# A hybrid decoder trunk on one core: the token tiles loaded first and by one queue, further expert rows fetched a chunk ahead, and a token's two expert rows summed on TensorE in the first layer

## The chip, the cores and the metric

The kernel runs on one core of a Trainium2 chip. The metric is the device time of one execution in microseconds (us), median over several executions. TensorE (PE), VectorE (DVE), ScalarE (ACT) and GpSimd (POOL) compute; SyncE (SP) issues most DMAs. "PEld" is the load of a matmul's stationary operand, PEclk the clock granted to TensorE as a share of 2.4 GHz. An fp32 matmul shows in the trace as two records.

## What is computed

One inference step of a two-layer trunk over 544 tokens (512 of a prompt, 32 of eight sample streams) with 1024 channels in fp32, cut to what matters here:

```python
for layer in (0, 1):
    h = rms_norm(x, g_mix[layer])
    x = x + (even_mixer(h) if layer == 0 else odd_mixer(h))  # attention + short conv; Conformer conv
    x = x + hier_moe(rms_norm(x, g_ffn[layer]))
y = rms_norm(x, g_final)

def hier_moe(x):          # top-1 of 4 groups, then top-2 of its 8 experts: 2 of 32 experts a token
    hg, hu = x @ w_gate[e], x @ w_up[e]                # 1024 -> 256 each
    act = silu(hg) * hu
    return sum(e_w[t, k] * (act @ w_down[e]) for k in (0, 1))     # 256 -> 1024, weights e_w
```

## The kernel before

Each engine has one program, and semaphores order them. The tokens stand in five tiles X[i] of 128, 128, 128, 128 and 32 rows by 1024 columns.

**Start.** ScalarE issues the five loads of X (line 808). SP issues the constants (503) and the gains and small weights (504), waits for three tiles, and then issues the first projection's weights (508 on). `norm(0)` then goes tile by tile: ScalarE sums squares (836), takes the root (838), VectorE inverts it (1104), ScalarE scales (842), TensorE turns eight 128x128 blocks (1748), VectorE keeps them with the gain (1113). TensorE's first projection (1768) needs three tiles.

**Experts** (one stage in each layer). Routing gives each of the 32 experts 64 places; a token beyond an expert's 64 goes to a *further chunk* of 64 places. The normed rows lie in DRAM (`xn_dram`). GpSimd gathers rows by an indirect DMA for two experts at a time (line 681; 765 and 708 for a further chunk, into `xe`), TensorE turns them (2120, chunk 2161), VectorE keeps them with the gain (1583, chunk 1613). Then for each expert: gate and up products (2137, chunk 2167), silu on ScalarE (949, chunk 970), product on VectorE (1594, chunk 1618), a turn on TensorE (2188, chunk 2171), its copy on VectorE (1601, chunk 1620), down products (2198, chunk 2176: four matmuls of 512 columns), a copy on ScalarE (958, chunk 974), and GpSimd writes the rows to their token's place in DRAM, by a copy of the index (739) and an indirect DMA (742). The chunks of expert u-1 stand on TensorE between its gate-and-up and those of expert u; their number is read at run time. SP streams the weights, 3 MB an expert, through six slots. A slot's gate and up part is loaded again (588) when the next expert's first product has begun (`gu_free`), its down part (592) when the down products are done. The first six experts' weights are loaded before the stage.

**After the experts.** ScalarE waits until all outputs are in DRAM (991), reads two counts (992) and signals SP, which loads each token's two expert rows, 2 x 1024 columns, tile by tile (604). In `combine` VectorE adds both, with their weights `cw`, into X, in two operations of 1024 columns a tile (1395). In the first layer `norm(2)` follows, whose updates run one tile ahead:

```python
                if ahead:
                    update(0)
                for s in range(TILES + 1):
                    if s < TILES:
                        ...
                        elif s + 1 < TILES:
                            update(order[s + 1])
                        dve.wait_ge(root_ready, TILES * call + s + 1)
                        nc.vector.reciprocal(...)      # gives ScalarE its scale for tile s
                    if s:
                        ...                            # keeps the turned halves of tile s - 1
```

TensorE turns tiles 0 to 2 with three filling matmuls (`stay_warm`, 1756) behind each of the first two, and then starts the odd mixer's first projection (2234). In the second layer the final norm (1722, 1723) follows and SP writes y (627).

What sets the order around the change is the order written in each engine's program, with the semaphores; there is no planner.

Of the kernel before, what the change touches and what calls it, by code (L numbers as in the profile page):

```python
# [24 lines left out]
I32 = mybir.dt.int32  # L25
ALU = mybir.AluOpType
# [3 lines left out]
P = 128  # L30
# [20 lines left out]
MSLOTS = SLOTS + 2  # L51
PIECE = 1024
# [85 lines left out]
def program(nc, x_in, w_mix0, kv_in, w_out, w_pw1, w_pw2, w_moe, smalls, consts, masks, rows, st_a, st_c,  # L138
            y_out, k_out, v_out, ua_p_out, ua_s_out, uc_p_out, uc_s_out):
    ctx = ExitStack()  # L140
    with ctx:
# [27 lines left out]
        tg = mb[:, 0:4 * MORE + 2].bitcast(I32)  # L169
# [14 lines left out]
        tile_in = [sem(f"tile_in_{i}") for i in range(TILES)]  # L184
        consts_in = sem("consts_in")
# [26 lines left out]
        ss_done = sem("ss_done")  # L212
# [3 lines left out]
        ss_turned = sem("ss_turned")  # L216
        ss_kept = sem("ss_kept")
        so_done = sem("so_done")
        so_sum = sem("so_sum")
        so_turned = sem("so_turned")  # L220
# [42 lines left out]
        class Moe:  # L263

            def __init__(self):
# [30 lines left out]
                self.combined = sem("combined")  # L296

        class Further:

            def __init__(self, n):  # L300
                self.ix = sem(f"ex_ix{n}")
                self.iy = sem(f"ex_iy{n}")
# [54 lines left out]
        sge, ave, aTe = (view(M_EXT + P * b, P) for b in range(3))  # L357
# [144 lines left out]
        def _(sp):  # L502
            sp.dma_start(cst[:, :], consts).then_inc(consts_in, 16)
            sp.dma_start(sv[:, :], smalls).then_inc(smalls_in, 16)

            for i in range(3):
                sp.wait_ge(tile_in[i], 16)
            sp.dma_start(ring[:, 0, 0:2 * D], w_mix0[0, :, 0:2 * D]).then_inc(later_w[0], 16)
            sp.dma_start(ring[:, 0, 2 * D:], w_mix0[0, :, 2 * D:]).then_inc(dense_w[0], 16)
            sp.dma_start(view(A_YT, 4 * P), masks).then_inc(masks_state_in, 16)  # L510
# [22 lines left out]
            def experts(n):  # L533
# [7 lines left out]
                if n == 0:  # L541
                    sp.wait_ge(so_done, 1)
# [90 lines left out]
        def _(pool):  # L633
# [3 lines left out]

            pool.wait_ge(smalls_in, 16)
# [32 lines left out]
            def experts(n):  # L671
# [28 lines left out]
                def chunk_rows(chunk):  # L700

                    pool.wait_ge(ex[n].turned, chunk + 1)
                    o = nc.s_assert_within(chunk + MORE, MORE, 2 * MORE,
                                           skip_runtime_bounds_check_because="at most MORE chunks and one empty")
                    nc.gpsimd.tensor_copy(ixe[0:JOB, 0:1], tg[0:JOB, bass.ds(o, 1)]).then_inc(ex[n].ix, 1)
                    pool.wait_ge(ex[n].ix, chunk + 1)
# [4 lines left out]
                def chunk_out(chunk):  # L711
# [4 lines left out]
                    nc.gpsimd.tensor_copy(ixy[:, 3:4], tb[:, bass.ds(o, 1)]).then_inc(ex[n].iy, 1)  # L716
# [1735 lines left out]
```

## Time and profile before

| | |
|---|---|
| runs | 1174.64 us median of 3 (1173.73 to 1178.26) |
| profiled execution | 1172.26 us, of it the span of the profile 1170.5 |
| busy | TensorE 88%, VectorE 37%, ScalarE 18%, GpSimd 16% of the span |
| DMA | 281.61 MB, mean 241 GB/s |
| mean granted TensorE clock | 0.949 |
| first projection, by the chain of waits | 18.70 us |
| experts of layer 1, first to last product | 328.21 to 565.20 us |
| first projection of the odd mixer | 592.83 us |
| experts of layer 2, first to last product | 883.82 to 1138.16 us |

The page gives the busy time of each engine, the span in 40 slices, the DMA queues, the chain of work that ended last, and the costliest groups of instructions. In a timeline or chain a row has the start and the duration in us, the engine, the line of the kernel, the operation and its operands (out<-in); "x8" is how many instructions are merged, and what stands in brackets is the engine's idle time before, with what ended it.

### The profile page before, as it was taken

To read this page: it belongs to the slowest core of one execution; us is meant where nothing else is said; L and a number is where in the kernel's file an instruction comes from. 1 tells how busy PE (TensorE), PEld (TensorE's weight loads), DVE (VectorE), ACT (ScalarE), POOL (GpSimd) and SP (SyncE) were. 2 spreads that over 40 slices of the span, in tenths; PEclk is the share of its full clock that TensorE was granted. 3 is DMA by queue.
4 is the path that set the end of the run, shared out by engine and by line. 5 is a ranking of instruction groups with operands and counts; after the bars stand their busy time and mean duration, and the time that the engine had idled before them with its cause. 6 is when DMAs were issued, how large, how long until landed. Compare 5 with 4: busy or idle time off the path is not lost.

```text
span 1170.5 us, 19147 instructions
## 1 busy us (share of the span) xinstructions
PE 1029.1 (88%) x7027; PEld 653.9 (56%) x7028; DVE 427.6 (37%) x904; ACT 209.6 (18%) x425; POOL 183.3 (16%) x282
## 2 busy tenths in 40 slices
PE   5999998879899978788399999988999998899980
PEld 4888786545555544444177767644565554555540
DVE  2542002454721111111349899454462111112116
ACT  4000112232201110011230101163120111111112
POOL 1000010000043222121112120110013222222120
PEclk9999999989999998899799999999979999999995
DMA  9424032345489999999642200264068999999915
GB/s 358 203 102 158 1 125 74 135 189 209 156 295 409 408 409 409 409 409 414 280 182 73 72 1 1 62 257 162 18 256 289 406 407 403 390 402 408 382 70 230
DMA packets 73776, 281.61 MB, mean 241 GB/s; under 512 B 12830, under 2 KB 13406, under 8 KB 70304
## 3 DMA queue, kind: packets, MB, share of 16 engines
q1 hardware_dynamic: 56992, 251.53, 54.8%
q0 software_dynamic: 10960, 17.89, 4.4%
q10 hardware_dynamic: 5744, 11.10, 2.8%
q8 instruction: 53, 0.87, 0.3%
q14 instruction: 27, 0.22, 0.1%
HBM read 270.23 MB, written 29.65 MB: 256 GB/s over the span
## 4 chain that ended last, share of the span: by engine, by line
PE 62%; DMA 20%; DVE 12%; ACT 3%; issue 2%; ACTq 0%; POOLq 0%; SPq 0%; POOL 0%; DVEq 0%
DMA ring<-w_moe 12%; PE psum L2137 11%; PE psum L2041 7%; DMA ar<-w_moe 6%; PE psum L2198 6%; PE psum L1812 5%; PE psum L1768 5%; PE psum L2234 5%; DVE ar L1671 5%; PE psum L2259 3%; PE psum L1881 2%; DVE X L1395 2%; PE psum L2120 2%; PE psum L2167 2%; PE psum L1879 1%
## 5 line engine op out<-in xcount | busy, mean ns | idle before, releaser
L2137 PE MATMUL psum<-ring,ar 128*64 128x256 f32 x1408 | 176.9, 396 | 18.2 <-DMA ring<-w_moe 16.3
L2137 PEld LDWEIGHTS psum<-ring,ar 128*64 128x64 f32 x1408 | 101.7, 142 | 89.9 <-issue 26.3
L2234 PE MATMUL psum<-ar,ring 128*128 128x272 f32 x512 | 121.3, 398 | 5.3 <-DVE ar L1657 2.9
L2234 PEld LDWEIGHTS psum<-ar,ring 128*128 128x128 f32 x512 | 97.6, 192 | 30.2 <-issue 4.2
L1671 DVE SCALAR_TENSOR_TENSOR ar<-ar,sv 128x512 f32<-128x512 f32 x120 | 107.0, 893 | 5.8 <-ACT ar L1025 1.9
L1601 DVE COPY ar<-psum 128x128 f32<-128x128 f32 x64 | 18.7, 292 | 245.0 <-PE psum L2188 245.0
L2041 PE MATMUL psum<-ring,ar 128*128 128x512 f32 x192 | 90.6, 622 | 4.7 <-DVE ar L1385 4.7
L2137 PE MATMUL psum<-ar 128*64 128x256 f32 x640 | 81.5, 399 | 8.1 <-DMA ar<-w_moe 8.1
L2198 PE MATMUL psum<-ring,ar 128*64 128x512 f32 x352 | 84.1, 598 | 0.8 <-DVE ar L1601 0.4
L742 POOL DMA_INDIRECT expert_outputs<-ar,ixy x64 | 63.9, 998 | 55.4 <-POOL ixy L739 55.4
L2137 PEld LDWEIGHTS psum<-ar 128*64 128x64 f32 x640 | 45.9, 143 | 42.4 <-issue 12.1
L949 ACT ACTIVATE ar<-psum 128x128 f32<-128x128 f32 x64 | 17.8, 278 | 281.0 <-PE psum L2137 281.0
L1768 PE MATMUL psum<-ar,ring 128*128 128x272 f32 x256 | 61.6, 402 | 2.0 <-DVE ar L1113 2.0
L2041 PEld LDWEIGHTS psum<-ring,ar 128*128 128x128 f32 x192 | 36.8, 199 | 45.8 <-issue 45.6
L958 ACT ACTIVATE ar<-psum 128x512 f32<-128x512 f32 x64 | 38.2, 597 | 132.0 <-PE psum L2198 132.0
L1768 PEld LDWEIGHTS psum<-ar,ring 128*128 128x128 f32 x256 | 49.3, 194 | 12.9 <-DVE ar L1113 2.4
L1594 DVE TENSOR_TENSOR ar<-ar,psum 128x128 f32<-128x128 f32 x64 | 18.4, 288 | 98.8 <-ACT ar L949 98.8
L1583 DVE TENSOR_TENSOR ar<-psum,sv 128x512 f32<-128x512 f32 x64 | 41.2, 686 | 24.1 <-PE psum L2120 24.1
L2198 PEld LDWEIGHTS psum<-ring,ar 128*64 128x64 f32 x352 | 23.3, 136 | 31.9 <-issue 25.1
L1812 PE MATMUL psum<-ar,ring 128*128 128x272 f32 x160 | 38.3, 392 | 0.0
L2198 PE MATMUL psum<-ar 128*64 128x512 f32 x160 | 38.2, 598 | 0.0
L2120 PEld LDWEIGHTS psum<-cst,ar 128*128 128x128 f32 x256 | 31.1, 193 | 12.1 <-issue 11.5
(262 smaller groups left out, 1188.2 us busy)
## 6 DMA issues: line engine op xcount, KB each, us to landing
ring<-w_moe SPq DMA_DIRECT2D x44, 2048.0 KB, 16.6
ring<-w_moe SPq DMA_DIRECT2D x44, 1024.0 KB, 18.1
ar<-w_moe SPq DMA_DIRECT2D x20, 2048.0 KB, 16.5
ar<-w_moe SPq DMA_DIRECT2D x20, 1024.0 KB, 17.1
ring<-w_pw SPq DMA_DIRECT2D x6, 2048.0 KB, 10.6
ring<-w_mix SPq DMA_DIRECT2D x3, 3072.0 KB, 23.9
ring<-expert_outputs SPq DMA_DIRECT2D x8, 1024.0 KB, 7.8
ring<-kv_in SPq DMA_DIRECT2D x2, 2880.0 KB, 11.3
```

The costliest lines, as they stand in the source:

```text
L742: pool.indirect_dma_start(ys_dram, bass.IndirectOffsetOnAxis(ixy[:, b:b + 1], 0), yj[b], None, bounds_check=4 * TOK - 1, oob_is_err=False) ...
L958: nc.scalar.activation(yj[b], psum[:, 4 + u % 2, :], ACT.Copy).then_inc(moe.y_kept, 1)
L1583: nc.vector.tensor_tensor(xt[:, 4 * h:4 * h + 4, :], psum[:, 3 + 4 * h, :].rearrange("p (k t) -> p k t", k=4), bcast(g[:, :, None], [P, 4, ...
L1671: t = nc.vector.scalar_tensor_tensor(out=out, in0=src, scalar=w, in1=out, op0=ALU.mult, op1=ALU.add)
L1768: t = mm(psum[:, proj_bank(m) + h, 0:HALF], w[:, k, :], hT[:, k, HALF * h:HALF * h + HALF], start=k == 0, stop=k == KD - 1)
L1812: t = mm(psum[:, mix_bank(q, what), 0:HALF], w[:, k, :], x[:, k, :], start=k == 0, stop=k == 3)
L2041: t = mm(psum[0:r, b + h, :], src[:, k, P * i:P * i + r], weights(k, h), start=k == 0, stop=k == blocks - 1)
L2120: t = tr(psum[:, 3 + 4 * (k // 4), o:o + P], rows_[:, k, :], ident)
L2137: t = mm(psum[64 * f:64 * f + 64, u % 2, 0:2 * P], xt[:, k, 64 * (u % 2):64 * (u % 2) + 64], w[:, k, f, :], start=k == 0, stop=k == KD - 1)
L2198: t = mm(psum[64 * h:64 * h + 64, 4 + u % 2, :], aT[:, 64 * k:64 * k + 64], slot(u % MSLOTS)[:, o:o + 512], start=k == 0, stop=k == 1)
L2234: t = mm(psum[:, glu_bank(m) + h, 0:HALF], w[:, k, o:o + P], hT2[:, k, HALF * h:HALF * h + HALF], start=k == 0, stop=k == KD - 1)
L2259: t = mm(psum[32 * s:32 * s + 32, 4 + i, :], diags(n)[32 * i:32 * i + 32, j, :], cu[32 * i:32 * i + 32, c, j:j + SEQ], start=j < 4, stop=j ...
```

## The change

It has these parts, in the order of the run:

- SP issues the five tiles of X, with the first 384 columns of the constants behind tile 0 and the gains of the norms (32 columns) behind tile 1; the weights' first load no longer waits for tiles. The rest of constants and small weights comes behind the first weights.
- The rows of further chunks: gathered and turned one chunk ahead. Chunk 0 is turned before expert 1, in every layer; each chunk turns the next one's rows behind its gate and up products and its activations through another bank. GpSimd's gather of chunk 0 moves ahead of the third pair's memset and gather.
- GpSimd takes the index of the last eight experts' outputs straight from the table.
- ScalarE reads the two counts before it waits for the outputs.
- The fetch of tile 0 is split into its two halves, in both layers.
- In the first layer VectorE makes ten diagonal matrices of the weights `cw`, TensorE multiplies each tile's two expert rows by them and sums them in PSUM, and VectorE adds the sum to X, for a tile of 128 rows in one operation. The fillings between the turns go; 22 stand ahead of the first sum.
- Two pairs of semaphores are merged, which changes no order.

The diff, cut to its core:

```diff
@@ sync
-            sp.dma_start(cst[:, :], consts).then_inc(consts_in, 16)
-            sp.dma_start(sv[:, :], smalls).then_inc(smalls_in, 16)
-
-            for i in range(3):
-                sp.wait_ge(tile_in[i], 16)
+            def tokens_in(i):
+                sp.dma_start(X[0:ROWS[i], i, :], x_in[P * i:P * i + ROWS[i], :]).then_inc(tile_in[i], 16)
+
+            tokens_in(0)
+            sp.dma_start(cst[:, 0:C_SM], consts[:, 0:C_SM]).then_inc(ident_in, 16)
+            tokens_in(1)
+            sp.dma_start(sv[:, 0:V_GPK], smalls[:, 0:V_GPK]).then_inc(gains_in, 16)
+            tokens_in(2)
             sp.dma_start(ring[:, 0, 0:2 * D], w_mix0[0, :, 0:2 * D]).then_inc(later_w[0], 16)
+            tokens_in(3)
+            tokens_in(4)
             sp.dma_start(ring[:, 0, 2 * D:], w_mix0[0, :, 2 * D:]).then_inc(dense_w[0], 16)
+            sp.dma_start(cst[:, C_SM:], consts[:, C_SM:]).then_inc(consts_in, 16)
+            sp.dma_start(sv[:, V_GPK:], smalls[:, V_GPK:]).then_inc(smalls_in, 16)
@@ sync, fetch
-                    sp.dma_start(yg[i][0:ROWS[i], :], src).then_inc(tile_in[i], 16)
+                    if i == 0:
+                        sp.dma_start(yg[0][:, 0:D], src[:, 0:D]).then_inc(first_rows_in, 16)
+                        sp.dma_start(yg[0][:, D:], src[:, D:]).then_inc(tile_in[0], 16)
+                    else:
+                        sp.dma_start(yg[i][0:ROWS[i], :], src).then_inc(tile_in[i], 16)
@@ gpsimd, experts
                         with pool.Fori(0, chunks) as c:
-                            chunk_rows(before + c + 1)
+                            chunk_rows(before + c + 2)
                             chunk_out(before + c)
@@
+                    if known:
+                        index = tb[:, MSLOTS * it + u:MSLOTS * it + u + 1]
+                        pool.wait_ge(moe.y_kept, MSLOTS * it + (EXPERTS * n + u + 1))
+                    else:
...
+                    pool.indirect_dma_start(ys_dram, bass.IndirectOffsetOnAxis(index, 0), yj[b], None,
@@
                 first_rows(1)
-                nc.gpsimd.memset(xg[2], 0.0).then_inc(moe.rows_clear, 1)
-                first_rows(2)
                 nc.gpsimd.memset(xe, 0.0).then_inc(pool_link, 1)
...
+                nc.gpsimd.memset(xg[2], 0.0).then_inc(moe.rows_clear, 1)
+                first_rows(2)
                 rows_of(3, 6)
+                pool.wait_ge(ex[n].turned, 2)
+                nc.gpsimd.tensor_copy(ixe[0:JOB, 0:1], tg[0:JOB, MORE + 1:MORE + 2]).then_inc(ex[n].index, 1)
+                pool.wait_ge(ex[n].index, 2)
+                pool.indirect_dma_start(xe, None, xn_dram, bass.IndirectOffsetOnAxis(ixe[0:JOB, 0:1], 0),
+                                        bounds_check=TOK - 1, oob_is_err=False).then_inc(ex[n].rows, 16)
@@ scalar, experts
+                further_chunks, before_last = (act.value_load(jt[0:1, o:o + 1], min_val=0, max_val=MORE)
+                                               for o in (EXPERTS - 1, 2 * EXPERTS - 1))
                 for b in range(3):
                     act.wait_ge(moe.y_out[b], 16 * (n + 1) * len(range(b, EXPERTS, 3)))
-                further_chunks, before_last = (act.value_load(jt[0:1, o:o + 1], min_val=0, max_val=MORE)
-                                               for o in (EXPERTS - 1, 2 * EXPERTS - 1))
@@ vector, experts
+                def keep_more_rows(chunk):
+
+                    dve.wait_ge(ex[n].turned, chunk + 2)
+                    nc.vector.tensor_tensor(
+                        xeT, psum[:, 7, :].rearrange("p (k t) -> p k t", k=KD),
+                        bcast(sv[:, V_GPK + 8 * n:V_GPK + 8 * n + 8][:, :, None], [P, KD, JOB]), ALU.mult
+                        ).then_inc(ex[n].turns_kept, 1)
@@ vector, after the first layer's experts
-            norm(2, combine(0))
+            for i in range(TILES):
+                for k in range(2):
+                    nc.vector.tensor_scalar(weight_diag(i, k), ident[0:ROWS[i], 0:ROWS[i]],
+                                            cw[0:ROWS[i], ODD_ORDER.index(i), k:k + 1], None, ALU.mult
+                                            ).then_inc(moe.combined, 1)
+
+            def add_sums(i):
+                r = ROWS[i]
+                dve.wait_ge(moe.first_sums, i + 1)
+                if i < TILES - 1:
+                    b = sum_bank(i, 0)
+                    nc.vector.tensor_tensor(X[0:r, i, :], X[0:r, i, :],
+                                            psum[0:r, b:b + 2, :].rearrange("p h c -> p (h c)"), ALU.add
+                                            ).then_inc(x_updated, 1)
+                    return
...
+            norm(2, add_sums)
@@ tensor, experts
+                def turn_more_rows(chunk):
+
+                    pe.wait_ge(ex[n].rows, 16 * chunk + 16)
+                    pe.sem_inc(moe.seen, 1)
+                    rows_ = xe.rearrange("t (d k) -> t k d", k=KD)
+                    for k in range(KD):
+                        t = tr(psum[:, 7, JOB * k:JOB * k + JOB], rows_[:, k, :], ident[0:JOB, 0:JOB])
+                    t.then_inc(ex[n].turned, 1)
@@ tensor, a further chunk
-                            pe.wait_ge(moe.rows_kept, MSLOTS * it + (EXPERTS * n + 2 * min(u // 2 + 1 + u % 2, last)))
-                            pe.wait_ge(ex[n].rows, 16 * (before + c) + 16)
...
-                            t.then_inc(ex[n].turned, 1)
                             pe.wait_ge(ex[n].kept, before + c + 1)
                             pe.wait_ge(ex[n].turns_kept, before + c + 1)
...
                             t.then_inc(ex[n].gu, 1)
+
+                            pe.wait_ge(moe.rows_kept, MSLOTS * it + (EXPERTS * n + 2 * min(u // 2 + 1 + u % 2, last)))
+                            turn_more_rows(before + c + 1)
                             pe.wait_ge(ex[n].act, before + c + 1)
-                            tr(psum[:, 7, 0:P], ave, ident).then_inc(ex[n].at, 1)
+                            tr(psum[:, 2, P:2 * P], more_act(n, 1), ident).then_inc(ex[n].at, 1)
...
                             t.then_inc(ex[n].down, 1)
+                            pe.wait_ge(ex[n].turns_kept, before + c + 2)
@@ tensor, body of the experts
                             down_weights(it, u - 1)
+                            if first and u == 1:
+                                turn_more_rows(0)
+                                pe.wait_ge(ex[n].turns_kept, 1)
@@ tensor, after the first layer's experts
-            for i in range(3):
-                turn(2, i)
-                if i < 2:
-                    stay_warm(3, 6)
+            def expert_rows(i):
+                r = ROWS[i]
+                if i >= 2:
+                    pe.wait_ge(x_updated, i if i == TILES - 1 else i - 1)
+                for k in range(2):
+                    if i == 0 and k == 0:
+                        pe.wait_ge(first_rows_in, 16)
+                    else:
+                        pe.wait_ge(tile_in[i], 32)
+                    pe.wait_ge(moe.combined, 2 * i + k + 1)
+                    for h in range(2):
+                        o = D * k + 512 * h
+                        t = mm(psum[0:r, sum_bank(i, h), :], weight_diag(i, k), yg[i][0:r, o:o + 512],
+                               start=k == 0, stop=k == 1)
+                t.then_inc(moe.first_sums, 1)
+
+            stay_warm(22, 2)
+            expert_rows(0)
+            expert_rows(1)
+            turn(2, 0)
+            expert_rows(2)
+            turn(2, 1)
+            expert_rows(3)
+            turn(2, 2)
+            expert_rows(4)
             pe.wait_ge(hT_ready, 26)
```

## Rows read from the trace of the kernel before

**Rows 1.** The page: DMA busy tenths in 40 slices of 29.26 us.
```profile
DMA  9424032345489999999642200264068999999915
```

**Rows 2.** The chain of waits, 0 to 40 us: start, us, what.
```profile
1.23 9.04 DMA X<-x_in
...
12.00 1.15 ACT ar L842
...
14.75 1.15 ACT ar L842
...
18.70 5.62 PE psum L1768 x16
```

**Rows 3.** DMA issues: operands, engine, count, KB each, median us to landing.
```profile
ring<-w_mix SPq DMA_DIRECT2D x1, 1024.0 KB, 5.0
...
ar<-normed_rows,ixe POOLq DMA_INDIRECT x8, 6.0
```

**Rows 4.** The timeline, GpSimd and TensorE at the start of the first layer's experts.
```profile
324.76 0.98 POOL L757 MEMSET ar<- 128x1024 f32 x1
...
327.50 0.97 POOL L759 MEMSET ar<- 64x1024 f32 x1
...
328.21 5.83 PE L2137 MATMUL psum<-ring,ar 128*64 128x256 f32 x52 [0.94 <-DVE ar L1583]
...
329.61 0.99 POOL L765 DMA_INDIRECT ar<-normed_rows,ixe  x1 [0.83 <-POOL ixe L762]
```

**Rows 5.** The timeline, TensorE in three further chunks of the second layer.
```profile
966.87 1.07 PE L2161 MATMUL psum<-cst,ar 64*128 64x64 f32 x8 [1.65 <-DMA ar<-normed_rows,ixe]
...
968.81 5.01 PE L2167 MATMUL psum<-ar 128*64 128x256 f32 x32 [0.88 <-DVE ar L1613]
...
995.07 1.09 PE L2161 MATMUL psum<-cst,ar 64*128 64x64 f32 x8
...
997.04 3.67 PE L2167 MATMUL psum<-ring,ar 128*64 128x256 f32 x32 [0.87 <-DVE ar L1613]
...
1001.40 0.33 PE L2171 MATMUL psum<-cst,ar 128*128 128x128 f32 x1 [0.69 <-DVE ar L1618]
...
1003.88 2.33 PE L2137 MATMUL psum<-ring,ar 128*64 128x256 f32 x20
```

**Rows 6.** The timeline between the layers' experts and the odd mixer.
```profile
563.26 1.94 PE L2198 MATMUL psum<-ring,ar 128*64 128x512 f32 x8 [0.38 <-DVE ar L1601]
...
571.38 1.99 SPq L604 DMA_DIRECT2D ring<-expert_outputs  x4
...
581.24 2.59 DVE L1395 SCALAR_TENSOR_TENSOR X<-ring,cw,X 128x1024 f32<-128x1024 f32 x2
...
587.90 2.10 PE L1756 MATMUL psum<-cst 128*128 128x384 f32 x6
...
589.84 1.04 PE L1748 MATMUL psum<-cst,ar 128*128 128x128 f32 x8
...
592.83 3.93 PE L2234 MATMUL psum<-ar,ring 128*128 128x272 f32 x16 [1.96 <-DVE ar L1113]
```

**Rows 7.** The chain of waits, 810 to 820 us.
```profile
814.35 3.43 PE psum L2041 x8
```

**Rows 8.** Line 1138, an add of 512 columns from PSUM: ns min/median/max.
```profile
L1138 DVE TENSOR_TENSOR X<-X,psum x16: 679/687/689, 269.3 to 856.3; 128x512 f32<-128x512 f32 x16
```

**Rows 9.** The timeline, TensorE in the first layer's experts.
```profile
507.71 3.87 PE L2137 MATMUL psum<-ring,ar 128*64 128x256 f32 x20 [2.79 <-DMA ring<-w_moe]
...
556.82 2.38 PE L2137 MATMUL psum<-ring,ar 128*64 128x256 f32 x20 [2.09 <-DMA ring<-w_moe]
```

**Rows 10.** The chain of waits at the end of the second layer's experts.
```profile
1138.86 0.20 POOL ixy L739
...
1139.90 2.30 DMA expert_outputs<-ar,ixy
...
1143.46 4.71 DMA ring<-expert_outputs
```

More of the change, by code:

```diff
@@ L296, in __init__ @@
                 self.combined = sem("combined")
+                self.first_sums = sem("first_sums")
         class Further:
             def __init__(self, n):
[L301 to L302 removed]
+                self.index = sem(f"ex_index{n}")
                 self.rows = sem(f"ex_rows{n}")
@@ L356, in program, with more_act, weight_diag, sum_bank @@
         ye = cst[:, C_SM:C_SM + 512]
-        sge, ave, aTe = (view(M_EXT + P * b, P) for b in range(3))
+        def more_act(n, b):
+            return sv[:, V_RW + KD * 64 * n + P * b:V_RW + KD * 64 * n + P * b + P]
+        def weight_diag(i, k):
+            o = M_G + 2 * D + 2 * P * i + P * k
+            return ar[0:ROWS[i], o:o + ROWS[i]]
+        def sum_bank(i, h):
+            return 5 + 2 * h if i == TILES - 1 else 4 + 2 * (i % 2) + h
         def slot(u):
@@ L702, in chunk_rows @@
                     pool.wait_ge(ex[n].turned, chunk + 1)
[L703 to L706, printed above, removed]
+                    o = nc.s_assert_within(chunk + MORE, MORE, 2 * MORE + 1,
+                                           skip_runtime_bounds_check_because="at most MORE chunks and two empty")
+                    nc.gpsimd.tensor_copy(ixe[0:JOB, 0:1], tg[0:JOB, bass.ds(o, 1)]).then_inc(ex[n].index, 1)
+                    pool.wait_ge(ex[n].index, 2 * chunk - 1)
                     pool.sem_inc(moe.seen, 1)
@@ L749, in body @@
                             rows_of(3 * it + (u // 2 + 4), u + 8)
-                        outputs(it, u)
+                        outputs(it, u, not gathers)
                 first_rows(0)
@@ L806, in _ @@
         def _(act):
-            for i in range(TILES):
-                act.dma_start(X[0:ROWS[i], i, :], x_in[P * i:P * i + ROWS[i], :]).then_inc(tile_in[i], 16)
             links = [0]
@@ L1639, in _ @@
             experts(0)
-            norm(2, combine(0))
+            for i in range(TILES):
[13 more added lines that the diff above has]
+                for h in range(2):
+                    cols = slice(512 * h, 512 * h + 512)
+                    t = nc.vector.tensor_tensor(X[0:r, i, cols], X[0:r, i, cols], psum[0:r, sum_bank(i, h), :],
+                                                ALU.add)
+                t.then_inc(x_updated, 1)
+            norm(2, add_sums)
             def glu(c):
@@ L2207, in body @@
                             down_weights(it, u - 1)
+                            if first and u == 1:
+                                turn_more_rows(0)
+                                pe.wait_ge(ex[n].turns_kept, 1)
                             further(it, u - 1, 4 if jobs == MSLOTS else 1)
```

97 lines of the change are left out of this document (51 added, 46 removed).

## The prediction, made before the change was run

> **What bounds the kernel now.** I read the page first. In its row of 40 slices the DMA engines are full in two long stretches, one in each expert stage [rows 1]. Shares don't say what sets the end, so I read the chain of waits stage by stage. At the start it runs through the load of a token tile and ScalarE's norm to the first projection at 18.70 us [rows 2]. In the first layer's experts it is TensorE's for a short time and then the weights' DMA. Between the layers it is the output rows' DMA and VectorE. In the second layer's experts it is TensorE's all the time, and the DMA engines are idle in its last 25 us (slice 39) [rows 1]. At the end it is the last output DMA, a ScalarE hand-over, the fetch and VectorE. So each edit is priced by its stage.
>
> **Start.** Tile 1 landed at 10.27 us, and all waited for it. From there the tiles follow each other by 2.75 (12.00 to 14.75), and the first projection comes 8.4 later [rows 2]. The change issues the tiles on SP, with a 128x384 part of the constants and 128 bytes a partition of gains between them. 1024 KB took 5.0 us to land [rows 3]; 512 KB less are 1.3 less at the 409 GB/s of the full slices, so 3.7, and tile 0 is there at 4.5. ScalarE, which issues nothing now, is ready for it. Tile 1 is needed at 7.3 and there at about 6.3 (1.25 MB ahead of and in it). The projection starts at 4.5 + 2.75 + 8.4 = 15.7, not 18.7: **-3.0 us** (-1.5 if tile 1 still comes last, at most -4). SP's queue now carries the five tiles ahead of most weights, but these no longer wait for three tiles to land and come earlier. The rest of the constants, 1.1 MB behind 5.6 MB, needs 16.4 us and VectorE asks for it only behind its norm, past the first projection.
>
> **First layer's experts.** Rows of an expert's 65th and later tokens are now turned once before expert 1, whether there are any or not. GpSimd's gather of them moves ahead of a memset and a row DMA, by 327.50 - 324.76 = 2.74, from 329.61 to 326.87 [rows 4]; 6.0 to land [rows 3], 332.9. Expert 0's products end at 328.21 + 32/52 of 5.83 = 331.8 [rows 4]. Behind the rows TensorE turns (1.09) and waits for VectorE (0.88) [rows 5], so expert 1 starts 1.1 + 1.97 = 3.1 later. The release of the first weight slot hangs on it, and the weight loads carry the stage to its end. The slice was 8 tenths full, so about 1 us is caught up: **+2.0** (0 if the DMA catches up, 3.3 if it does not).
>
> **The sum on TensorE.** From the layer's last down-product (563.26 + 1.94 = 565.20) to the next projection at 592.83 are 27.6 us [rows 6]. Their place is taken, in TensorE's order, by:
> - 22 matmuls of 384 columns. Six records took 2.10 us [rows 6]; by the records of 512 columns, 0.43 each [rows 7], they are 0.32 each and a tail. An fp32 matmul is two records (the four down-products show as eight). So 14.1 us, and TensorE is free at 579.3. The fetch, issued at 571.38 before [rows 6], goes 1.9 earlier (see the ends of the layers), and its first half is there by 573: the rows wait for the filling.
> - Five sums of four matmuls of 512 columns, 3.43 us each [rows 7]. The tile of 32 rows costs the same.
> - The loop. VectorE's norm adds tile k+1 before it gives out tile k's inverse root, and TensorE takes up sum k+2 only behind the turn of tile k. So sum, add, inverse (0.2), scaling (1.15) [rows 2], turn (1.04) [rows 6] and 0.1 for their hand-overs stand in series. The add of 1024 columns from PSUM has no row: at least 1.29, half of the pair of updates of that width [rows 6], at most two adds of 512, 1.37 [rows 8]; I take 1.3. From the end of one sum to the start of the next 3.8.
>
> 14.1 + 2 x 3.43 + 3.8 + 2 x (3.43 + 3.8) + 3.43 + 2.8 (last add, inverse, keeping of two halves at 1.3) = 45.5: **+17.9**. VectorE does save 1.3 a tile. But a period of 3.9 on VectorE alone (2.59 for the updates, 1.3 for keeping) [rows 6] gives way to one of 7.2 through three engines. The ten diagonals are made while the rows are on their way and cost nothing; without that cover they would be ten small VectorE operations, about 2 us.
>
> **The clock.** Where TensorE had waited 2.79 us for weights it took 3.87 for twenty records, elsewhere behind 2.09 us only 2.38 [rows 9]: in the first case the granted clock was at 1.2 GHz for a part. In the new loop no sum runs for 3.8 us, three times. I add 1.5 for each, **+4.5** (0 to 3.4 each, the latter a whole sum at 1.2 GHz). The Trainium skill ("TensorE: Matmul & The Clock Gate", section "HAM oscillation") speaks against the change here: waits between short bursts of matmuls throttle every burst. The trace agrees with 1.49 us in one of the two waits; the rule at its hardest would make the time 5.7 longer. The same page (section "Back-to-back issue gap") has 216 ns for 512 columns, where our fp32 rows have 0.86 us for a matmul; by it the five sums would be 13 us cheaper. The measurement decides.
>
> The stage together: **+22.4**.
>
> **Second layer's experts.** Expert 1 is later here too, by the turning and its wait, the rows being there in time: **+2.0**. All six further chunks of 64 tokens are in this stage. One alone takes 995.07 to 1003.88 = 8.8 us: turning and wait 1.97, products 3.67, wait 0.69, then 2.48 for the activations' turn and the down-products [rows 5]. After the change the next chunk's turning (1.09) stands in the wait of 0.69: 3.67 + 1.09 + 2.48 = 7.24, less by 1.57, four times 6.3. VectorE's keeping of these rows (0.69) ends inside the down-products. The two chunks behind each other lost 1.65 more to the row DMA and 1.34 to a low clock [rows 5]: 20.6; now twice 7.24 and some 1.1 left of the DMA wait, 15.6: 5.0 less. Together **-11.3** (-8 to -13). The weights don't take it back, since they were all there 20 us before the end.
>
> **Ends of the layers.** The last eight output DMAs take their index straight from the table: 1138.81 to 1139.90, a copy and its wait, go. ScalarE reads its two counts before it waits: 0.9 of the 1.26 us from 1142.20 to 1143.46 go [rows 10]. In layer 1 both vanish behind the filling; in layer 2 **-1.9**. Halving tile 0's fetch starts VectorE 1.3 earlier, but tile 1's DMA comes no sooner and SP has one more issue: 0 (-1 to +0.5).
>
> **Sum.** -3.0 + 2.0 + 22.4 + 2.0 - 11.3 - 1.9 = **+10.2** on the profiled execution's 1172.26 us (span 1170.5): 1182.5. That execution is 2.4 under the median, 1174.64, so the forecast for the median is **1184.8 us**.
>
> **Rivals.**
> - *The clock holds and the DMA catches up in layer 1.* For it: the wait of 2.09 us that cost nothing [rows 9]. 1184.8 - 4.5 - 2.0 = 1178.3, within 0.5%.
> - *The clock stays at 1.2 GHz through the loop*: three sums late by 3.4 and not 1.5: 1190.5.
> - *The rows of the next chunk come late*, so that TensorE waits in the middle of a chunk instead of at its head: the 11.3 are lost, 1196. Against: in four of six the gather has more than an expert's time.
> - *Faster*: filling and sums cost half, if a record is a whole matmul. Then the filling ends before the rows come at 573, a sum is 1.7, the stage 31.4 (+3.8) and the total -8.4: 1174.6 - 8.4 = 1166. The change wins as soon as the stage costs under 14 us more. Against: the eight records of four down-products.
>
> **Chances.** Forecast 0.48, clock holds 0.26, clock low 0.12, rows late 0.06, faster 0.08. A measurement here tells about 0.5% (5.9 us) from nothing. Slower by more: 0.66; within: 0.26; faster: 0.08. The range, 1176 to 1192, leaves out the last two cases and takes in the bounds of clock and start.
>
> **What would show it.** Right: the first projection near 15.7; a filling of 14 us that ends after the rows have landed; three gaps of 3.8 us between sums with only turns in them; a chunk in 7.2 us; expert 1 of both layers 2 to 3 us later. Wrong: sums that follow each other by 4.5 us (no serial loop), a stage between the layers under 35 us, or a second expert stage no shorter than before.

## The result, and the profile after

The changed kernel takes **1197.77 us** in the median of six runs (1193.81 to 1201.48), the kernel before, beside it, 1176.23 (1170.95 to 1179.02). The ratio is 1.0193, with a 95% interval of 1.0168 to 1.0217: slower by 1.9%. The forecast was 1184.8 in a range of 1176 to 1192, so the sign was right and the size was not. The profiled execution of the changed kernel took 1198.0 us (span 1196.2), 25.7 more than that of before.

A table of seven stretches shows where. Each figure is the difference of two starts (or ends) of TensorE's rows in the timeline; the last column is the prediction's own change.

| stretch | before | after | change | predicted |
|---|---|---|---|---|
| start to first projection | 18.70 | 17.27 | -1.4 | -3.0 |
| from there to the first expert product, layer 1 | 309.51 | 310.96 | +1.4 | 0 |
| experts of layer 1, first product to end of last | 236.99 | 241.24 | +4.3 | +2.0 |
| between the layers, to the next projection | 27.63 | 50.00 | +22.4 | +22.4 |
| projection to first expert product, layer 2 | 290.99 | 295.82 | +4.8 | 0 |
| experts of layer 2 | 254.34 | 248.95 | -5.4 | -9.3 |
| last product to the end | 32.34 | 31.96 | -0.4 | -1.9 |

**Start.** The chain of waits of the changed kernel, 0 to 18 us, and below it ScalarE's row of that tile in the timeline (against [rows 2]):

```profile
3.63 10.71 DMA X<-x_in
...
17.27 0.82 PE psum L1837
```
```profile
14.36 1.06 ACT L870 ACTIVATE ar<-X 128x1024 f32<-128x1024 f32 x1 [1.44 <-DMA X<-x_in]
```

Tiles 0 to 2 came as forecast (ScalarE takes up tile 1 at 7.33, without a wait). The fourth did not: it is issued at 3.63, behind the first weights, and lands at 14.34; ScalarE waits 1.44 us for it. The projection doesn't read it, but VectorE gives out its inverse root before it keeps tile 2's turned halves, so the first projection waits for it. Without this wait it would have started at about 15.8, the 15.7 of the forecast.

**Layer 1, expert 1.** TensorE's timeline (against [rows 4]):

```profile
328.23 3.67 PE L2206 MATMUL psum<-ring,ar 128*64 128x256 f32 x32 [0.94 <-DVE ar L1624]
...
331.83 1.09 PE L2219 MATMUL psum<-cst,ar 64*128 64x64 f32 x8
335.08 2.38 PE L2206 MATMUL psum<-ring,ar 128*64 128x256 f32 x20 [2.16 <-issue]
```

VectorE's keeping ends at 332.97 + 0.69 = 333.66. Expert 1's products start 1.4 us behind that, and the row gives "issue" as the end of the wait: something on TensorE's own queue. Where in the kernel before only the wait stood between a chunk's turning and its products, TensorE idled 0.87 us [rows 5]; here it is 2.16. From the stage's first product to expert 1's there are 6.85 us, 3.3 more than before (3.59); 3.1 were forecast. That this fits is luck: of the forecast's 1.1 us of waiting for the rows nothing was spent (GpSimd issues their gather at 325.85, not 326.87, and it lands after 2.1 us, not 6.0), and the 1.4 took its place.

**Between the layers.** TensorE's timeline, whole (against [rows 6]), and VectorE's rows of one round of the loop:

```profile
569.40 14.46 PE L1825 MATMUL psum<-cst 128*128 128x384 f32 x44
583.69 7.03 PE L2328 MATMUL psum<-ring,ar 128*128 128x512 f32 x16
593.29 1.78 PE L1817 MATMUL psum<-cst,ar 128*128 128x128 f32 x8 [2.57 <-ACT ar L876]
594.86 4.64 PE L2328 MATMUL psum<-ring,ar 128*128 128x512 f32 x8
602.07 1.09 PE L1817 MATMUL psum<-cst,ar 128*128 128x128 f32 x8 [2.57 <-ACT ar L876]
603.00 3.60 PE L2328 MATMUL psum<-ring,ar 128*128 128x512 f32 x8
609.17 1.09 PE L1817 MATMUL psum<-cst,ar 128*128 128x128 f32 x8 [2.57 <-ACT ar L876]
610.19 6.66 PE L2328 MATMUL psum<-ar 32*32 32x512 f32 x8
619.47 3.09 PE L2312 MATMUL psum<-ar,ring 128*128 128x272 f32 x6 [2.62 <-DVE ar L1147]
```
```profile
599.54 1.22 DVE L1700 TENSOR_TENSOR X<-X,psum 128x1024 f32<-128x1024 f32 x1 [7.48 <-PE psum L2328]
600.67 0.16 DVE L1138 RECIPROCAL stat<-stat 128x1 f32<-128x1 f32 x1
600.75 1.27 DVE L1147 TENSOR_TENSOR ar<-psum,sv 128x512 f32<-128x512 f32 x2
```

This is the serial loop of the forecast. From sum to sum at full clock it is 610.19 - 603.00 = 7.19 us, 7.2 forecast (3.60 for the sum and 3.59 of gap, where 3.43 and 3.8 were taken). The add takes 1.22 (1.3 taken). The sum of the 32-row tile takes 6.66 instead of 3.60, and the projection behind it 6.28 instead of 3.93: the windows view (stretch, its length, TensorE's busy time and records, granted clock, DMA share, GB/s) has the granted clock at 0.53 in 612 to 625 us, close to the lower of the two levels (1.2 of 2.4 GHz).

```profile
612.00:625.00 13.00, 10.38 (x20) 0.53 0.00 0
```

**Layer 2.** The start of the experts in the chain of waits, then GpSimd's gather of the first chunk's rows, expert 1's first twenty products and one further chunk in the timeline (against [rows 5]):

```profile
915.29 3.67 PE psum L2206 x32
918.96 1.07 issue
920.03 1.08 PE psum L2219 x8
921.11 0.02 issue
921.13 0.70 DVE ar L1647
921.83 1.05 issue
```
```profile
912.81 0.98 POOL L794 DMA_INDIRECT ar<-normed_rows,ixe  x1 [0.84 <-POOL ixe L791]
...
922.88 4.54 PE L2206 MATMUL psum<-ring,ar 128*64 128x256 f32 x20 [1.79 <-issue]
...
1028.46 3.62 PE L2238 MATMUL psum<-ring,ar 128*64 128x256 f32 x32
1032.02 1.09 PE L2219 MATMUL psum<-cst,ar 64*128 64x64 f32 x8
1033.04 0.33 PE L2245 MATMUL psum<-cst,sv 128*128 128x128 f32 x1
1033.75 1.94 PE L2250 MATMUL psum<-ring,sv 128*64 128x512 f32 x8 [0.38 <-DVE sv L1665]
1035.52 2.33 PE L2206 MATMUL psum<-ring,ar 128*64 128x256 f32 x20
```

A single chunk takes 1035.52 - 1028.46 = 7.06 (7.24 forecast, 8.8 before). The pair takes 16.3 us (15.6 forecast), 4.5 less than before. With 1.85 for each of the four single ones (1.75 in the chunk, 0.1 in the products ahead of it) the chunks give back 11.9 us, and 6.5 of these are lost again at expert 1: 1.07 until the rows' turning starts, 1.08 + 0.70 for turning and keeping, 1.05 behind it, 2.2 by expert 1's first twenty products, which take 4.54 us and not 2.33, and the rest by slower records right behind them. The 1.07 is the rows' landing, although the chain calls it "issue": their gather took 7.1 us from its issue at 912.81, so to 919.9, and the turning starts at 920.03. Two other kernels show the same (6.8 us from 886.0 and a turning at 892.88 in e8, 7.6 us from 909.1 and 916.85 in e3).

**End.** The chain of waits (against [rows 10]):

```profile
1164.91 0.03 POOLq L773
1164.94 0.49 issue
1165.43 0.22 POOLq L142
1165.65 2.52 DMA expert_outputs<-ar,tb
...
1168.38 0.34 SPq L626
...
1168.75 0.43 SPq L627
...
1169.23 7.19 DMA ring<-expert_outputs
```

Without the index copy the output DMA still needs 0.77 us from the end of ScalarE's copy to its start; 1.1 before. From SP's first issue of the fetch to the end of VectorE's last row there are now 25.37 us, 24.63 before.

### The profile page after: what moved, and what is told of

Read it like the earlier page. It is cut to its first block, busy times and chain, and to the rows that moved or that the text cites. A ratio compares the mean times of both kernels' runs of the same rounds, so it can differ in the third digit from the quotient of the medians.

```text
span 1196.2 us, 19357 instructions
## 1 busy us (share of the span) xinstructions
PE 1071.5 (90%) x7115; PEld 673.1 (56%) x7116; DVE 424.0 (35%) x912; ACT 209.5 (18%) x425; POOL 182.6 (15%) x270
## 4 chain that ended last, share of the span: by engine, by line
PE 65%; DMA 19%; DVE 11%; ACT 2%; issue 2%; SPq 0%; POOLq 0%; DVEq 0%; POOL 0%; ACTq 0%
PE psum L2206 11%; DMA ring<-w_moe 11%; PE psum L2110 7%; DMA ar<-w_moe 6%; PE psum L2273 6%; PE psum L1881 5%; PE psum L2312 5%; PE psum L1837 5%; DVE ar L1740 5%; PE psum L2358 3%; PE psum L1825 3%; PE psum L1950 2%; PE psum L2328 2%; PE psum L2189 2%; PE psum L2238 1%
## 5 line engine op out<-in xcount | busy, mean ns | idle before, releaser
L1642 DVE COPY ar<-psum 128x128 f32<-128x128 f32 x64 | 18.7, 292 | 249.0 <-PE psum L2263 249.0
L773 POOL DMA_INDIRECT expert_outputs<-ar,ixy x48 | 48.1, 1002 | 41.5 <-POOL ixy L770 41.5
L1825 PE MATMUL psum<-cst 128*128 128x384 f32 x114 | 46.0, 559 | 0.0
```

The source lines that it names most:

```text
L773: pool.indirect_dma_start(ys_dram, bass.IndirectOffsetOnAxis(index, 0), yj[b], None, bounds_check=4 * TOK - 1, oob_is_err=False).then_inc( ...
L1825: mm(psum[:, bank, 0:C_SM], ident, cst[:, 0:C_SM], start=True, stop=True)
```

## The experiments

Theory after the result: four costs beside the stage. (1) The first wait for the kept rows holds up TensorE's sequencer. (2) The start's gain is bound to a late tile. (3) The split fetch costs an issue. (4) The clock falls behind the new stage. The rival to all: these are scatter or contention, and the stage is the only cost. Each kernel was run beside the kernel before; ratios are to that.

**e1: the old update between the layers, all else as changed.**

```diff
-            norm(2, add_sums)
+            norm(2, combine(0))
...
-            stay_warm(22, 2)
-            expert_rows(0)
...
+            for i in range(3):
+                turn(2, i)
+                if i < 2:
+                    stay_warm(3, 6)
```

> The changed kernel with one part undone: between the layers VectorE again adds both expert rows in two operations a tile, with the three fillings behind the first two turns; all other edits kept. Theory A (the sum on TensorE is the loss, and the clock behind it): the stage goes from 50.0 us back to about 27.6, the projection behind it from 6.28 to about 3.9, and the second layer's first expert product comes no later than before, so 22 to 27 us less than after, 1171 to 1176, within 0.5% of before. Theory B (the loss sits in the further rows' turning and in contention, the stage alone is given back later): at most 15 less, above 1182.

Measured: 1172.25 us, ratio 0.9973 (0.9946 to 1.0001). That is 25.5 less than after; the stage is 28.3 again. Theory A, but two of its points failed: the projection behind the stage took 5.62 and not 3.9, and the first expert product of layer 2 came at 895.89, 12 us later than before. Of these 1.0 lie ahead of layer 1's experts, 6.3 in them, 0.7 in the stage and 4.1 behind it; the shorter second stage makes up for 5.9 of them. This profiled execution, 1177.83 us, lies 5.6 above the kernel's median.

**e2: the sum on TensorE alone in the kernel before.** The same edit the other way.

> The kernel before with the sum on TensorE alone (diagonals, sums, adds, 22 fillings; the fetch not split, the two semaphores of the turned samples merged to make room, which changes no order). Theory A: the stage 49 to 51 us, the clock behind it low for some us, 22 to 27 us slower than before, that is 1198 to 1203. Theory B (the sum alone costs only its 17.9 of work, the clock falls for other reasons): 1193 to 1195 and the projection behind it at 3.9 to 4.5 us.

Measured: 1201.43 us, ratio 1.0229 (1.0181 to 1.0277), 24.6 above before. Its stage takes 49.65, its experts 237.5 and 254.4 as before, the stretch behind the stage 296.6. So from both sides the sum costs about 25 us in medians, 22 of them in the stage. Where the other 3 lie the profiles don't tell: behind the stage e2 has 5.6 more than before, and after only 0.7 more than e1. All the other edits together are worth about -4 us, inside the scatter.

**e3: the wait behind expert 1's products.**

```diff
                             if first and u == 1:
                                 turn_more_rows(0)
-                                pe.wait_ge(ex[n].turns_kept, 1)
                             further(it, u - 1, 4 if jobs == MSLOTS else 1)
                         gate_up(it, u, first)
+                        if first and u == 1:
+                            pe.wait_ge(ex[n].turns_kept, 1)
```

> The changed kernel with one wait moved: TensorE waits for VectorE's keeping of the first further rows behind expert 1's gate and up products, not ahead of the loop over expert 0's chunks. Theory A (the wait holds up the sequencer, which reads the chunk count and branches only behind it): expert 1 starts about 1.9 us earlier in each layer, and in the second layer its products run at 2.33 and not at 4.54 us, because the engine stood still for less: 2 to 6 us less than after, 1192 to 1195. Theory B (the turning itself is the cost): no more than 1 us less.

Measured: 1189.57 us, ratio 1.0115 (1.0068 to 1.0162), 8.2 less than after in the medians (3.8 between the profiled spans). TensorE's timeline in layer 1:

```profile
331.78 1.09 PE L2219 MATMUL psum<-cst,ar 64*128 64x64 f32 x8
332.80 2.38 PE L2206 MATMUL psum<-ring,ar 128*64 128x256 f32 x20
```

Expert 1 follows the turning at once. Ahead of the loop over chunks TensorE's program reads their number and branches, and nothing else stands there; with the wait in front of it this could begin only when the rows were kept. That it is these instructions is read from the program; that the place of the wait costs the time is measured. Theory A, with more than its upper bound in the medians: expert 1 starts 2.2 us earlier after the first product, and the experts of layer 1 take 238.15 and not 241.24. The table of all kernels below bears this out. In layer 2 theory A failed in this profile: expert 1's first twenty products take 3.98 and not 2.33, the rows land later still (1.43 of waiting ahead of their turning), and a chunk's last down products take 3.63 instead of 1.94.

**e5: the norm not one tile ahead.**

```diff
-                ahead = call == 2
+                ahead = False
```

> The changed kernel with the norm behind the sum no longer one tile ahead: VectorE adds tile s, gives out its inverse, and only then adds tile s+1. Theory A (the loop is serial because the turn of tile k waits for the add of tile k+1): sum, turn, sum follow each other at 4.5 to 5 us and not at 7.2, the stage is 7 to 8 us shorter, TensorE waits for less than 1.5 us at a time, so the clock falls less too: 7 to 11 less than after, 1187 to 1191. Theory B (the period is set by TensorE and VectorE work alone): 0 to 2 less.

Measured: 1183.97 us, ratio 1.0070 (1.0038 to 1.0103), 13.8 less than after. TensorE's timeline:

```profile
594.86 1.09 PE L1817 MATMUL psum<-cst,ar 128*128 128x128 f32 x8 [0.77 <-ACT ar L876]
595.79 3.60 PE L2328 MATMUL psum<-ring,ar 128*128 128x512 f32 x8
599.23 1.04 PE L1817 MATMUL psum<-cst,ar 128*128 128x128 f32 x8
600.10 3.60 PE L2328 MATMUL psum<-ring,ar 128*128 128x512 f32 x8
603.59 1.09 PE L1817 MATMUL psum<-cst,ar 128*128 128x128 f32 x8
605.01 3.62 PE L2328 MATMUL psum<-ar 32*32 32x512 f32 x8 [0.33 <-DVE X L1700]
608.56 5.57 PE L2312 MATMUL psum<-ar,ring 128*128 128x272 f32 x16
```

A round takes 600.10 - 595.79 = 4.3. The stage is 35.7 and not 50.0, a gain of 14.3 where theory A has 7 to 8: the wait of 2.6 ahead of the projection goes too, since tile 2 is kept while the last sum runs, and all sums run at full clock. With the sum on TensorE "one tile ahead" closes a ring through three engines; whether it still pays with the update on VectorE alone was not tried. One thing stays unexplained: the projection takes 5.57 us, 3.93 at full clock, though TensorE had waited no longer than 0.77 us at a time since the fillings.

**e6: e5 with 10 fillings and not 22.** (`stay_warm(22, 2)` becomes `stay_warm(10, 2)`.)

> The changed kernel with the norm not ahead, as in e5, and 10 fillings ahead of the first sum and not 22. Theory A (the filling holds up sums whose rows are there): the filling ends at about 576, the rows of tile 0 land 5.3 + 4.7 and 5.3 + 8.3 us behind the last down product as in the trace of after, so the first two sums end 3 to 4 us earlier than in e5: 1180 to 1181 by e5's 1183.97. Theory B (TensorE idles while the rows come, the clock falls and the sums run longer): what is won is given back, 1182 to 1186. Either way slower than before, since 22 us of sums and turns stay where 3 turns stood.

Measured: 1179.21 us, ratio 1.0025 (0.9998 to 1.0052), 4.8 less than e5. TensorE's timeline:

```profile
580.25 8.83 PE L2328 MATMUL psum<-ring,ar 128*128 128x512 f32 x16 [2.75 <-DMA ring<-expert_outputs]
```

The stage is 32.7: 3.0 less than in e5, at the lower end of theory A. TensorE waits 2.75 us for the rows behind the filling, and theory B has its share: the granted clock is 0.65 from 580 to 584 us, and the first two sums take 8.83 together, 7.03 in e5. The projection behind the stage runs at full clock (3.93), unlike e5's, from which this kernel differs by twelve fillings ahead of the first sum.

**e7: fillings in the loop.** `stay_warm(3, b)` ahead of each of the turns 0 to 2.

> The changed kernel with three filling matmuls (2.1 us) ahead of each of the turns 0 to 2 in the loop of sums, where TensorE waits 2.57 us. Theory A (the clock fell because TensorE waited in each round): the sums all take 3.5 us, the last one too (6.66 in after), the projection behind them 3.9 to 5: 3 to 6 us less than after, 1192 to 1195. Theory B (the clock would fall in any case): the same as after, 1197 to 1199, with the last sum and the projection still over 6 us. The serial period stays 7.2 us under both.

Measured: 1189.89 us, ratio 1.0115 (1.0071 to 1.0158), 7.9 less than after, more than theory A's 3 to 6 and more than the stage gives. TensorE's timeline:

```profile
598.40 2.10 PE L1825 MATMUL psum<-cst 128*128 128x384 f32 x6
601.13 1.09 PE L1817 MATMUL psum<-cst,ar 128*128 128x128 f32 x8 [0.63 <-ACT ar L876]
602.06 3.60 PE L2328 MATMUL psum<-ring,ar 128*128 128x512 f32 x8
605.50 2.10 PE L1825 MATMUL psum<-cst 128*128 128x384 f32 x6
608.23 1.09 PE L1817 MATMUL psum<-cst,ar 128*128 128x128 f32 x8 [0.63 <-ACT ar L876]
609.25 3.62 PE L2328 MATMUL psum<-ar 32*32 32x512 f32 x8
615.49 6.01 PE L2312 MATMUL psum<-ar,ring 128*128 128x272 f32 x16 [2.63 <-DVE ar L1147]
```

The stage takes 45.3 instead of 50.0, every sum 3.6, the granted clock is 1.00 up to 612 us. So the clock cost 4.7 us inside the stage, and filling TensorE's waits brought them back. The projection, behind an unfilled wait of 2.63, still takes 6.01, so that part of theory A failed.

**e9: the new start alone in the kernel before.**

> The kernel before with the new start alone (tiles and constants on SP; two pairs of semaphores merged, which changes no order). Theory A (the start wins 1.4 us up to the first projection and the clock behind it takes some back): first projection at 17.0 to 17.3 and not 18.70, the fourth tile landing near 14.3, the first expert product at 326.5 to 328.2. Theory B (the gain is kept): first expert product at 326.5 or earlier. The time itself is within the scatter of before in both.

Measured: 1178.13 us, one run. The first projection starts at 16.91 (-1.8), the first expert product at 329.11 (+0.9, outside both theories). Against before, row by row, the lead of 1.8 holds until 196 us. There six groups of two to four records take 0.54 to 1.16 us each, 0.32 to 0.63 before, and by 211 us the lead is gone. Of 0.7 that come back later the twelve filling records ahead of the experts, 6.48 us and not 4.88, take 1.6. The first of the slow ones, in the chain of waits:

```profile
196.47 0.61 PE psum L1933 x2
197.08 1.15 PE psum L1941 x4
```

And with a stage of 27.7, as before, the stretch behind it still takes 294.5 and not 291.0.

**e8: e1 and e3 together.**

> The changed kernel with two parts undone or moved: the old update between the layers, as in e1, and TensorE's wait for the first further rows behind expert 1's products, as in e3. Theory A (the two costs are independent, 25 and about 7 us with the clock): 5 to 8 us less than e1, which measured 1172.25, so 1164 to 1167, faster than before by 0.7 to 1.0%, with the first layer's experts 238 us from first product to last and not 243. Theory B (what e3 gave back came from the state of the clock behind the sums): the same as e1, 1171 to 1173.

Measured: 1166.81 us, ratio 0.9928 (0.9903 to 0.9953): faster than both kernels. Layer 1's experts take 238.3, as theory A says, layer 2's 244.5.

**e10: e8, with the fourth tile ahead of the first weights.** `tokens_in(3)` moves up one line.

> e8 with the fourth token tile issued ahead of the first weights on SP. Theory A (the tile landed late, at 14.6, because 1 MB of weights stood ahead of it, and VectorE's order passed this on to the third tile's keeping): it lands before 12.8, the first projection starts at 15.5 to 16.2, not at 17.57. Theory B (the queue's rate sets it, or the weights come late in its place): 16.8 or later. The time within the scatter of e8.

Measured: 1166.19 us, one run. ScalarE takes up the tile without a wait at 13.55 (14.65 in e8, behind a wait of 0.67), and the first projection starts at 16.45, 1.1 earlier, between the two theories: 0.25 outside A's numbers and 0.35 outside B's. A's mechanism holds, since the wait for the fourth tile is gone; what keeps the start from 15.7 is tile 1, which ScalarE takes up at 8.05 here, 8.39 in e8 and 7.33 in after. With e13, whose projection starts at 16.17, the two kernels with the fourth tile first are ahead of all ten with the weights first (16.78 to 17.57). Whether the gain lasts is not shown: the first expert product starts at 325.48, not 328.83, but in e12, with e8's start unchanged, it starts at 326.00, and the stretch from the first projection to it scatters from 309.0 to 312.4 us over the kernels with SP's start.

**e12: e8, with tile 0 fetched in one DMA again.**

> e8 with the first tile's fetch in one DMA again. Theory A (the half costs SP one more issue, and tile 1 lands no sooner): from the first fetch's issue to the end of the run 24.6 us as in before, 0.7 to 0.9 less than with the split. Theory B (the split lets VectorE start 1.3 us earlier and keeps it): 0.5 or more longer than with the split. The time within the scatter of e8.

Measured: 1167.78 us, one run. From SP's first issue to the last row's end 24.70 us; 25.37 in e8, as in after, and 24.63 before. Theory A: the split costs 0.7 at the end (0.4 by e13, which also fetches in one DMA and takes 24.98).

**e11: e6 and e3 together, the sum on TensorE at its best.**

> The changed kernel with the sum on TensorE kept, the norm behind it not ahead, 10 fillings, and TensorE's wait for the first further rows behind expert 1's products: e6 and e3 together. Theory A (the costs add up): 5 to 8 us less than e6, which measured 1179.21, so 1171 to 1174, within 0.5% below before but 4 to 7 us above e8, which differs from it by the update alone. Theory B (the wait's cost was bound to the clock behind a long stage of sums): 1177 to 1180.

Measured: 1171.08 us, ratio 0.9968 (0.9946 to 0.9989), 8.1 less than e6. The stage takes 32.9, with 27.6 in e8 from the same end of layer 1 (566.94 and 567.11). So the sum still costs 5 us of stage against the update on VectorE, 4.3 in the medians.

**e13: e8, e10, e12 and 22 fillings ahead of the first turn.**

> e8 (the changed kernel with the old update and the late wait, 1166.81) with three more edits: the fourth token tile issued ahead of the first weights, the first tile's fetch in one DMA again, and 22 fillings ahead of the first turn between the layers. Theory A (each gives what its row shows): first projection at 15.5 to 16.2 and not 17.57, 0.7 less at each layer's fetch, the first turn between the layers 1.1 and not 1.97 us and the projection behind it at full clock; by the sum 2 to 4 less than e8, 1163 to 1165. Theory B (the start's gain is eaten by the clock in the attention stage as before, and the fillings change only where the clock falls next): 1166 to 1168.

Measured: **1163.57 us**, ratio 0.9904 (0.9877 to 0.9930), the fastest kernel here, though its interval overlaps that of e8. The time is theory A's, but its part on the fillings failed. They did nothing: TensorE's timeline has a wait behind them and the same slow first turn as in e8 (1.97 for eight records).

```profile
564.61 14.46 PE L1795 MATMUL psum<-cst 128*128 128x384 f32 x44
582.92 1.97 PE L1787 MATMUL psum<-cst,ar 128*128 128x128 f32 x8 [3.86 <-ACT ar L872]
```

**The expert stages of all kernels**, in us from first product to the end of the last down products, from their timelines:

| kernels | layer 1 | layer 2 |
|---|---|---|
| old chunks: before, e2, e9 | 237.0, 237.5, 238.3 | 254.3, 254.4, 254.4 |
| new chunks, wait ahead: after, e1, e5, e6, e7 | 241.2, 243.3, 243.4, 242.1, 243.2 | 249.0, 248.4, 248.7, 249.0, 248.8 |
| new chunks, late wait: e3, e8, e10, e11, e12, e13 | 238.2, 238.3, 239.0, 238.2, 237.9, 238.2 | 248.5, 244.5, 244.5, 244.7, 248.2, 245.4 |

In layer 1 no kernel with new chunks and the wait ahead is under 241.2 and none without over 239.0: 3 to 5 us for one wait of 0.7 us with a count behind it. The prefetch itself costs layer 1 no more than about 1 us, within the spread of the old chunks. In layer 2 it gives 10 us where the clock holds.

## Why the prediction missed

**Right.** The sign, and the stage between the layers to the tenth: 50.0 us. Its parts stand too: filling 14.46, five sums, rounds of 7.2, and 45.5 of work against 45.3 in e7, where the clock held; 4.5 for the clock against 4.7. In this last term only the sum is right, and that by luck: 1.5 were put to each round, and 1.7, 0 and 3.1 came (1.7, 0 and 2.7 in e2, 1.7, 0 and 3.3 in e3). The Trainium skill ("TensorE: Matmul & The Clock Gate", section "HAM oscillation") speaks of throttling in every round; the trace agrees in the first round (0.7 + 1.0 more for turn and sum) and in the third (3.1), not in the second; the rule's hardest form, 5.7 on top of the 4.5, is not borne out. Two inner steps were off without effect: counted from the last down product the fetch was issued 0.8 earlier, not 1.9, and tile 0's first half landed 10.0 behind it, not 7.8, the second 14.0 behind, at 583.5. The filling ended just then and hid that too. The chunks gave 11.9 against 11.3.

**Wrong, by the terms of the sum**, for the profiled executions (25.7 against 10.2, so 15.5 to explain):

- *"Expert 1 is later here too, by the turning and its wait", +2.0 in each layer.* +4.3 in layer 1, +6.5 in layer 2: 6.8 missing. The step counted the turning and VectorE's keeping, and not what stood behind the wait on the same queue: the read of a count and a branch, 1.4 and 1.05 us, which had been hidden while matmuls ran. The prediction asked what hangs on expert 1's start for the weights' release, but not what stands behind this wait. In layer 1 the 1.4 was offset by rows for which there was no wait, where 1.1 us had been put down; there the step failed at its end, where "about 1 us is caught up": expert 1 started 3.3 late and the stage ended 4.3 late, so nothing was caught up. In layer 2 the rest is the half clock behind the wait and the 1.07 until the rows had landed, which "the rows being there in time" denied. e3 and the table show what the wait's place costs, 3 us in layer 1 alone. The Trainium skill ("Perfetto Trace Analysis", section "Sequencer-only Instruction (DRAIN, etc)") says that a sequencer fetches its next instruction only after a waiting control instruction is through, and that this wait is in no row. The trace agrees as far as it goes: products behind the wait start late, and the 1.4 and 1.05 appear only as "issue"; how they divide among the read, the comparison and the branch no row shows.
- *"**-3.0 us**" at the start.* 1.4 at the first projection, 0 at the experts. The step set the tiles' landing by the queue's bytes but looked at tiles 0 to 2 alone; the fourth, behind 1 MB of weights, was on the path by VectorE's order (1.44 in after, 0.67 in e8, nothing in e10). What was gained did not reach the experts: in e9, compared row by row, records at half clock took it; whether the same holds for after was not followed row by row.
- *Nothing behind the stage.* +4.8. It had no term. 2.35 of it is the projection itself, 6.28 and not 3.93, and only part of the whole is the change's: with the old update between the layers e8 has +2.9 there, e9 +3.5 and e1, e10 and e12 +4.1, while before's profiled execution, 2.4 under the median of its first three, has the shortest of all. That the sum alone (e2) costs 24.6 in medians leaves 2 to 3 us for it.
- *Ends, -1.9.* -0.4. GpSimd's 1.1 became 0.77 and not near nothing, the output DMA took 0.2 more, and the split fetch, costed at 0, costs 0.7 (e12). ScalarE's counts were right (1143.46 - 1142.20 = 1.26 before, 0.21 after).
- *Chunks*: 0.6 more than forecast.

3.0 + 6.8 + 4.8 + 1.5 - 0.6 = 15.5. In medians the miss is 13.

**The rivals.** "The clock holds and the DMA catches up" fell: layer 1 never caught up, each kernel with the wait ahead ends it 4 to 6 us late. "The clock stays at 1.2 GHz" was nearer, 1190.5, but for a reason in the loop, while the missing time lay elsewhere. The range held only clock and start, since expert 1 was given bounds of 0 to 3.3 from the DMA's side alone. The rival "faster if the stage costs under 14 us more" was never tried as such, but its threshold did not hold (by the prediction's own terms it is 12.2 and not 14, and that rival's stage sums to 30.6 and not 31.4): with the stage at +8.1 (e5) and +5.1 (e6) the kernel was not faster, since the other edits gave 4 us and not 12. With the late wait it is, just, at +5.2 (e11).

What stays open: how the 2.2 us by which the wait delays expert 1 in layer 1 become 3.1 at the end of the stage (after against e3), and why in other kernels, as e1, a half clock of another 2.2 us comes on top. How much of +4.8 the stage causes. And what makes the granted clock fall where no wait above 0.77 us stands ahead, as in e5.

## What to carry to other kernels

Moving an addition from VectorE to TensorE saved VectorE 1.3 us a tile and cost 22 us, of which 17 came from an order ("one tile ahead") and a filling that the new split of the work did not need; ask for both before such a move. Ahead of a semaphore wait look at what follows on the same queue even where it does no work: here the reading of a count and a branch cost nothing while matmuls were still running, and 1.0 to 1.4 us behind a wait. And don't count on a DMA-bound stage to catch up: here 2.2 us more at its head came out as 3.1 at its end, and as 5 where half clock came on top.

## What the runs showed of the hardware

- Where TensorE's granted clock falls is not the same in kernels with the same code there. In layer 2 of e12 and e8, which differ only in the fetch of tile 0 behind each layer, the same eight down products took 3.48 and 1.94 us (behind waits of 0.38 and 0.39), and the first twenty products of expert 1 took 4.05 and 2.38. These two places are 3.2 of the 3.7 us by which the two expert stages differ, so a single profile of each can't tell such kernels apart.
- 14.5 us of filling ahead of a wait of 3.86 us did not keep the next eight matmuls fast (e13: 1.97, as without any). Filling the wait itself did (e7).
- The last output's indirect DMA started 0.77 us behind the end of ScalarE's copy with the index ready in the table; the copy of the index was worth only 0.33.
